# Output projection's steps spread around the last recurrent head, one memory key pair ahead of a norm, rotary work in pairs

## What is computed

```python
for i in range(2):                       # first block
    a = rms_norm(h, pre_mix_norm[i])
    m = hgrn2_mixer(a, ...) if i == 0 else mla_mixer(a, ...)
    h = h + rms_norm(m, post_mix_norm[i])
    f = squared_relu_mlp(rms_norm(h, pre_mlp_norm[i]), w_mlp_in[i], w_mlp_out[i])
    h = h + rms_norm(f, post_mlp_norm[i])
    e = p[i] @ w_ple_proj[i]             # the "embedding" of layer i
    h = h + rms_norm(sigmoid(h @ w_ple_gate[i]) * e, ple_norm[i])
# second block: hybrid mixer, cross attention to mem (256 rows), gated conv MLP
# hgrn2_mixer, per head of 8: q, two forget gates, v, output gate; a chunked scan both ways,
#   o = rms_norm(o_f + o_b) * silu(gate); then the heads together @ w_out
# mla_mixer: cq, ckv, k_rope = split(x @ w_in); cq, ckv normed
#   q = cq @ w_uq -> 16 heads of 128 + 64 rotary columns; k, v = ckv @ w_ukv
#   softmax(q_nope k_nope + q_rope k_rope) v, then the 16 heads @ w_o
```

## Time and profile before

| | |
|---|---|
| median of 3 runs (2368.69 to 2370.6) | 2370.27 us |
| the profiled execution's own time | 2372.49 us |
| its span | 2370.6 us |
| PE, share of the span busy | 97% |
| DVE, ACT, POOL | 54%, 27%, 66% |
| mean granted clock of PE | 0.989 |

### The profile page before, as it was taken

How to read it: one execution, slowest core, us unless ns; L and a number is a source line. 1 busy time by engine, 2 the same in 40 slices (tenths; PEclk the granted TensorE clock), 3 DMA queues, 4 the chain that set the end, 5 groups by cost and what they waited for, 6 DMA issues and landing times.

```text
span 2370.6 us, 27451 instructions
## 1 busy us (share of the span) xinstructions
PE 2291.2 (97%) x10372; PEld 1857.8 (78%) x10372; DVE 1271.2 (54%) x1820; ACT 648.5 (27%) x1190; POOL 1568.0 (66%) x1530
## 2 busy tenths in 40 slices
PE   7999989999999899999999999999999999999998
PEld 6888877888887677777778888878767787888886
DVE  6674727145245666256372454458875444626354
ACT  3343433101013345245231010132345232202112
POOL 7556556877776545544668777769425947878784
PEclk9999999999999899999999999999999999999999
DMA  5222222333332211211324333323212322333332
GB/s 162 76 71 80 72 79 73 112 97 97 98 98 76 59 35 36 71 42 32 97 73 128 98 99 111 98 76 116 71 37 80 111 67 89 96 97 97 98 96 73
DMA packets 110868, 200.13 MB, mean 84 GB/s; under 512 B 12305, under 2 KB 18705, under 8 KB 110737
## 3 DMA queue, kind: packets, MB, share of 16 engines
q1 hardware_dynamic: 107568, 194.72, 27.4%
q10 hardware_dynamic: 3168, 3.67, 0.5%
HBM read 196.24 MB, written 2.10 MB: 84 GB/s over the span
## 4 chain that ended last, share of the span: by engine, by line
PE 87%; DVE 6%; POOL 4%; ACT 2%; issue 1%; DMA 0%; SPq 0%; DVEq 0%; POOLq 0%
PE bank L469 26%; PE bank L471 25%; PE bank L470 25%; POOL wL L2612 2%; POOL wH L2610 1%; DVE bank L1834 1%; DVE h L1826 1%; PE bank L998 1%; PE bank L502 1%; PE bank L864 1%; DVE tmp L1826 1%; PE bank L869 1%; PE bank L870 1%; PE bank L865 1%; PE bank L866 1%
## 5 line engine op out<-in xcount | busy, mean ns | idle before, releaser
L2612 POOL TENSOR_TENSOR wL<-raw,wH 128x512 fp32r<-128x512 f32 (+2 forms) x731 | 1000.7, 1369 | 60.9
L2610 POOL TENSOR_SCALAR wH<-raw 128x512 fp32r<-128x512 f32 (+2 forms) x731 | 531.2, 727 | 616.4 <-PE bank L471 523.6
L469 PE MATMUL bank<-aH,wH 128*128 128x512 f32 x1376 | 547.0, 398 | 19.2 <-DVE aL L1834 9.6
L471 PE MATMUL bank<-aH,wL 128*128 128x512 f32 x1376 | 537.5, 391 | 0.0
L470 PE MATMUL bank<-aL,wH 128*128 128x512 f32 x1376 | 537.4, 391 | 0.0
L469 PE MATMUL bank<-uH,wH 128*128 128x512 f32 x960 | 375.7, 391 | 5.6 <-DVE uL L1826 5.6
L470 PE MATMUL bank<-uL,wH 128*128 128x512 f32 x960 | 374.5, 390 | 0.0
L471 PE MATMUL bank<-uH,wL 128*128 128x512 f32 x960 | 374.5, 390 | 0.0
L469 PEld LDWEIGHTS bank<-aH,wH 128*128 128x128 f32 x1376 | 258.9, 188 | 78.7 <-issue 13.1
L470 PEld LDWEIGHTS bank<-aL,wH 128*128 128x128 f32 x1376 | 259.0, 188 | 57.0 <-issue 4.1
L471 PEld LDWEIGHTS bank<-aH,wL 128*128 128x128 f32 x1376 | 258.9, 188 | 54.7
(11 more groups left out here) (315 smaller groups left out, 3202.3 us busy)
## 6 DMA issues: line engine op xcount, KB each, us to landing
raw<-in_ws SPq DMA_DIRECT2D x699, 256.0 KB, 2.6
raw<-in_ws SPq DMA_DIRECT2D x24, 192.0 KB, 2.3
h<-in_xT SPq DMA_DIRECT2D x4, 512.0 KB, 7.3
E<-in_memT ACTq DMA_DIRECT2D x16, 128.0 KB, 2.6
out<-c_F SPq DMA_DIRECT2D x8, 256.0 KB, 2.1
tmp<-in_pT ACTq DMA_DIRECT2D x4, 256.0 KB, 3.2
raw<-in_ws SPq DMA_DIRECT2D x8, 128.0 KB, 2.1
g_hc<-in_cst SPq DMA_DIRECT2D x1, 640.0 KB, 9.2
```

The costliest lines, as they stand in the source:

```text
L469: P.e.matmul(o, lH, rH, start=start, stop=False, skip_group_check=skip)
L471: return P.e.matmul(o, lL, rH, start=False, stop=stop, skip_group_check=skip)
L2610: G.e.tensor_scalar(H, x, 1.0, 0.0, MUL, ADD).then_inc(*G.did("wH", n))
L2612: G.e.tensor_tensor(L, x, H.bitcast(F32), SUB).then_inc(*G.did("w", n))
```

## The change

For head 7, one step of the output projection stands ahead of `recur(7)`, two ahead of `outputs(7)`, one behind it, and four behind the sum of squares; ACT loads the Exp table right after the last Sigmoid, ahead of its part of `recur(7)`. At the end of both embeddings tile 7 is squared by DVE; in layer 1 `memory_keys(0)` stands ahead of `stat_end` and `memory_keys(2)` behind it. In the attention's start, ACT squares the query latent into `m_P` and DVE adds the squares there, so the key latent's norm and the query latent's sum interleave; all `normed` run one tile ahead of their low halves; the rotary key comes last. `values_in(0)` stands ahead of the duplication; the query of head 0 ahead of its key; the rotary columns of heads 2 and 3 ahead of `scores(0)`, whose four banks are taken at once, all parts without rotary columns first. Rotary pairs come in odd iterations, one iteration earlier; `rotate` on DVE is cut in two, `rotate` and `rotated`, the latter in the next iteration, and `m_qr` is double buffered. Head 8's query, key and scores stand ahead of `mla_out(0)`, and the keys of heads 8 and 9 come as pieces of their own.

```diff
--- before.py
+++ after.py
     def keys(hd):
-        add("mla_w_ukv", 0, (0, 1), ((256 * hd, 128), (256 * hd + 256, 128)))
+        if hd in (8, 9):
+            add("mla_w_ukv", 0, (0, 1), cols((256 * hd, 128)))
+        elif hd % 2 == 0:
+            add("mla_w_ukv", 0, (0, 1), ((256 * hd, 128), (256 * hd + 256, 128)))
...
     values(0)
-    keys(0)
     rope(0)
     query(0)
+    keys(0)
+    rope(2)
     for hd in range(16):
...
-        if hd % 2 == 0 and hd < 14:
-            rope(hd + 2)
+        if hd % 2 and hd < 12:
+            rope(hd + 3)
         if hd % 8 == 7:
-            divided[len(out) + 1] = hd - 1
-            divided[len(out) + 5] = hd
-            mla_out(hd // 8)
+            divided[len(out) + (hd == 15)] = hd - 1
             if hd == 7:
                 head(8)
+            divided[len(out) + (5 if hd == 15 else 2)] = hd
+            mla_out(hd // 8)
...
                     lin = three_open([("hg_w_out", 0, 128 * o) for o in range(3)], ...
-                    for k in range(5):
-                        three_step(lin, k, uH, uL, y1_ready)
+                    out_steps(0)
                 recur(head)
                 if head < 7:
                     project(head + 1, 0)
                 else:
-                    three_step(lin, 5, uH, uL, y1_ready)
-                    three_step(lin, 6, uH, uL, y1_ready)
+                    out_steps(1, 2)
                 outputs(head)
                 if head < 7:
                     project(head + 1, 3)
+                else:
+                    out_steps(3)
                 stat_end("hs", head, tiles=1, tail=False, freed=(V, "on", head))
...
-            three_step(lin, 7, uH, uL, y1_ready)
+            out_steps(4, 5, 6, 7)
...
+                if i == 1:
+                    memory_keys(0)
                 stat_end("ple", i, adds=f"n{i}")
                 P.also("end ple", i)
                 if i == 1:
-                    for o in (0, 2):
-                        memory_keys(o)
+                    memory_keys(2)
...
+            values_in(0)
             b1, b2 = take("kr1"), take("kr2")
...
-            values_in(0)
-            key_in(0)
             rope_in(0)
             query_in(0)
             rotate(0)
+            key_in(0)
+            rope_in(2)
             scores(0)
             for hd in range(16):
-                ahead, turn = hd % 8 != 7, hd % 2 == 0 and hd < 14
+                ahead, turn = hd % 8 != 7, hd % 2 == 1 and hd < 12
                 if ahead:
                     heads_in(hd + 1)
                 if turn:
-                    rope_in(hd + 2)
+                    rope_in(hd + 3)
                 turned(hd)
                 if ahead:
                     scores(hd + 1)
+                elif hd == 7:
+                    heads_in(8)
                 if turn:
-                    rotate(hd + 2)
+                    rotate(hd + 3)
+                elif hd == 0:
+                    rotate(2)
                 values(hd)
                 if hd == 7:
+                    scores(8)
                     mla_out(0)
-                    heads_in(8)
-                    scores(8)
...
                 sigmoid_g(head)
                 if head < 7:
                     sigmoid_f(head + 1, 1)
+                else:
+                    exp_table()
                 recur(head)
...
-                    if o == 7:
-                        exp_table()
-                    A.wait_ge(V, "Fg", i, o)
-                    square(("ple", i), o, F[:, o, :])
+                    if o < 7:
+                        A.wait_ge(V, "Fg", i, o)
+                        square(("ple", i), o, F[:, o, :])
+                exp_table()
...
+                V.wait_ge(V, "Fg", i, 7)
+                V.wait_ge(V, "sum", ("ple", i), 6)
+                tt(sq[:, :], F[:, 7, :], F[:, 7, :], MUL).then_inc(*V.did("sq", ("ple", i), 7))
...
+            add_query_squares(1)
+            normed(3)
+            add_query_squares(2)
+            normed(4)
+            normed_low(3)
+            normed_low(4)
             V.wait_ge(P, "kr")
             tt(F[0:64, 5, :], bk("kr")[0:64, :], r[0:64, :], MUL).then_inc(*V.did("kr"))
-            for k in range(3):
-                normed(k, turned_key(k))
...
+            normed(0)
+            normed(1)
+            normed_low(0)
+            normed(2)
+            normed_low(1)
+            normed_low(2)
+            turned_key()
```

More of the change, by code:

```diff
@@ L366, in build @@
             m_qnH, m_qnL, m_knH, m_knL = (sb(n, [128, T], FR, st) for n in ("m_qnH", "m_qnL", "m_knH", "m_knL"))
-            m_qr = [sb(f"m_qr{i}", [128, T], FR, st) for i in range(2)]
+            m_qr = [[sb(f"m_qr{j}{i}", [128, T], FR, st) for i in range(2)] for j in range(2)]
             m_P = [sb(f"m_P{i}", [128, 4, T], F32, st) for i in range(2)]
@@ L815, in pe @@
             P.also("n0 used")
-            stat_end("cq", tiles=3, tail=False, freed=(V, "cn", 2))
+            b = take("stat", "cq")
+            P.wait_ge(V, "sum", ("cq",))
+            P.e.matmul(b.ap[:, :], ones, m_P[0][:, 0, :], start=True, stop=True).then_inc(*P.did("stat", "cq"))
+            give(b, V, "cn", 2)
             aVH, aVL, aPH, aPL = aH[:, 0:4, :], aL[:, 0:4, :], aH[:, 4:8, :], aL[:, 4:8, :]
@@ L1473, in act, with query_square @@
                 square(("ckv",), k, F[:, 3 + k, :])
-            rstd(256, "ckv")
+            def query_square(k):
+                A.wait_ge(V, "lat", k)
+                do(m_P[0][:, k, :], F[:, k, :], ACT.Square).then_inc(*A.did("sq", ("cq",), k))
             def latent(k):
@@ L1478, in latent @@
                 do(m_cH[:, k, :], tmp[k % 2][:, :], ACT.Copy).then_inc(*A.did("cH", k))
[L1480 to L1484 removed]
+            query_square(0)
+            query_square(1)
+            rstd(256, "ckv")
+            query_square(2)
+            latent(3)
+            latent(4)
             rstd(384, "cq")
@@ L1497, in values_in, with key_high @@
                     do(aVH[:, t, :], bk("mV", quad, t)[:, :], ACT.Copy).then_inc(*A.did("mVH", quad, t))
+            def key_high():
+                A.wait_ge(V, "kr3")
+                do(m_krH[:, :], F[:, 6, :], ACT.Copy).then_inc(*A.did("krH"))
             def rope_in(hd):
@@ L1549, in act @@
             values_in(0)
-            head_in(0, "kn", m_knH)
+            key_high()
             rope_in(0)
             head_in(0, "qn", m_qnH)
-            rotate(0)
-            A.also("rope done")
+            head_in(0, "kn", m_knH)
+            rotated(0)
             scores(0)
+            rope_in(2)
             for hd in range(16):
-                ahead, turn = hd % 8 != 7, hd % 2 == 0 and hd < 14
+                ahead, turn = hd % 8 != 7, hd % 2 == 1 and hd < 12
                 if ahead:
@@ L1564, in act @@
                     scores(hd + 1)
-                if turn:
-                    rotate(hd + 2)
+                elif hd == 7:
+                    heads_in(8)
+                if hd % 2 == 0 and 0 < hd < 14:
+                    rotated(hd + 2)
                 values(hd)
+                if hd == 0:
+                    rotated(2)
                 if hd == 7:
+                    scores(8)
                     A.wait_ge(V, "krL")
@@ L2271, in dve @@
             values_in(0)
-            head_in(0, "kn", m_knH, m_knL)
+            V.wait_ge(A, "krH")
+            low(m_krL[:, :], F[:, 6, :], m_krH[:, :]).then_inc(*V.did("krL"))
             head_in(0, "qn", m_qnH, m_qnL)
             rotate(0)
+            head_in(0, "kn", m_knH, m_knL)
+            rotated(0)
             scores(0)
             for hd in range(16):
-                ahead, turn = hd % 8 != 7, hd % 2 == 0 and hd < 14
+                ahead, turn = hd % 8 != 7, hd % 2 == 1 and hd < 12
                 if ahead:
@@ L2282, in dve @@
                     scores(hd + 1)
+                elif hd == 7:
+                    heads_in(8)
                 if turn:
-                    rotate(hd + 2)
+                    rotate(hd + 3)
+                elif hd == 0:
+                    rotate(2)
+                elif hd % 2 == 0 and hd < 14:
+                    rotated(hd + 2)
                 values(hd)
+                if hd == 0:
+                    rotated(2)
                 if hd == 7:
-                    heads_in(8)
                     scores(8)
```

117 lines of the change are left out of this document (62 added, 55 removed).

## The result

The changed kernel takes 2339.21 us (median of 4 runs, 2337.48 to 2340.41), the kernel before 2370.43 beside it (2368.69 to 2372.69): ratio 0.9867, 95% interval 0.985 to 0.9884, so 31 us less. The forecast was 2340.5. The profiled execution took 2338.12 (span 2336.3, mean granted clock 0.994) against 2372.49 before.

A forecast was written before the change was run, and what follows sets the result against it. PE bounds the kernel, busy 2291 of 2371 us, so only its waits and half-clock time can be won. Terms 3.4 - 0.3 + 14.0 + 6.3 + 5.9 + 0.5 = 29.8 us gave a 2340.5 us median; range 2332 to 2350.

The forecast's parts named there:

- Step 1: End of the recurrence: two PE waits and their half clock go, a new 4.1 us wait comes; net gain 3.4 us.
- Step 2: Square of the embeddings' last tile, on DVE in layer 0: 0.1 us gain to 0.7 loss, taken as 0.3 lost.
- Step 3: Attention's start: PE's waits and half clock, 14.8 us together, go against 0.8 us of new waits; net gain 14.0 us.
- Steps 4 and 5: Head loop: waits for `m_knL` in odd iterations shrink, gain 6.3 us; iteration 7's wait and half clock go, gain 5.9.
- step 5: Iteration 7: `values(7)`'s 4.3 us wait and 1.6 of clock loss go, by head 8's matmuls and no preceding `m_qr`; 5.9 us.
- Step 6: Second embedding: `memory_keys(0)` covers the square's wait, but POOL's splits set PE's restart; gain 0.5 us, bounds -1.5 and +1.
- B: Attention's start: DVE's chain is slower beside POOL's splits, `knL` 4 us later; 2347 us, chance 0.11.
- C: Attention's start: fp32 products, not waits, cause the low clock, so 5.0 us are not won; 2345.5 us, chance 0.11.
- D: POOL's divisions come later behind regrouped splits, delaying each `turned(hd)`; slower, 2379.5 us at 7 us each, chance 0.02.
- E: No change: head 7's new wait and the head loop's shifted ones return all but iteration 7; 2366 to 2370 us, chance 0.03.

The follow-up runs named there:

- square_alone: The changed kernel with one GpSimd weight piece in layer 0's embedding waiting for DVE's last-tile square; first embedding's stage 71.24 us against 72.97.
- table_later: The changed kernel with ACT's Exp table load behind its part of `recur(7)`; wait for `g_kT` 3.99 to 2.57 us, recurrence's stage 1.42 us shorter.
- steps_3_1_1_3: The changed kernel with the later Exp table load and output projection steps 3 | 1 | 1 | 3; recurrence's stage 76.3 us against 81.4.
- steps_alone: The changed kernel with output projection steps 3 | 1 | 1 | 3 and nothing else; recurrence's stage 76.52 us, 4.85 less.
- rec_only: The kernel before with only the change of the recurrence's end; 2368.13 us against 2371.69.
- values_behind: The changed kernel with PE's `values_in(0)` behind the two duplications of the rotary key; attention's stage 357.90 us, to the hundredth the changed kernel's.
- rotate_whole: The changed kernel with `rotated` right behind the rotation in odd iterations, not one iteration later; attention's stage 4.1 us longer.
- head8_late: The changed kernel with head 8's query, key and scores behind the first output projection again; attention's stage 1.97 us longer.
- keys_behind: The changed kernel with both `memory_keys` behind the second embedding's sum; second embedding's stage 175.49 us, ratio to the kernel before 0.9875.

## Why the prediction was right, step by step

The sum was 29.8 us, the medians moved by 31.2 and the profiled executions by 34.4, of which 1.9 lie ahead of any edit.

- **Step 1, 3.4, measured 4.0.** The wait is there as worked out (4.1, measured 3.99), for `g_kT`, with the table load ahead of the copy; the waits for the sum and for `uL` are gone. The clock cost 1.7 instead of 2.1 (the window of 0.57: low for 3.44 of 4 us). In three of the nine executions with this stage as in after it cost 1.1 to 1.3 more, so 2.7 to 4.0 is the part's worth, against the one R of before.
- **Step 2, -0.3, measured -1.5. This is the term that was mis-sized.** The square was placed right (763.03, behind the product) and its duration was within the bounds (1.64, upper bound 1.70), but of the two neighbouring rows the loss was taken near the middle. The rows part the 1.5: PE's wait for the square grew from 1.77 to 2.38 us, which is 0.6 and inside the forecast's bound of 0.7; and the clock fell ahead of two fp32 products, which took 2.02 us for 1.12, 0.9 more. The term had no clock in it at all. In `square_alone` both are gone; in `table_later`, `steps_3_1_1_3` and `steps_alone` the 0.6 stays and the 0.9 doesn't come, with the same square.
- **Step 3, 14.0, measured 15.2 or 14.4.** `turned(0)` starts at 853.05 before and 833.46 after, 19.6 less, of which 4.4 stand already at the landmark before it. Against `rec_only`, where the clock fell later, it is 14.4. Half clock and waits went as forecast, and of the 0.8 us of new waits only 0.2 came (`m_P`, at `turned(0)`), since DVE was ahead: `knL` ended at 825.06, when the first score was issued at 825.37. `values_behind` corrects the reason: the forecast credited `values_in(0)` with hiding the query latent's chain, and behind the duplications it hides as much.
- **Steps 4 and 5, 12.2, measured 14.0.** The places were right, all seven waits for `m_knL` and the one for `aL` are gone. The size was low because a wait costs more than its row: three waits of 3.4 us in `rotate_whole` cost A 4.1, one of 1.5 in `head8_late` cost 2.0. The products come every 0.23 us but their rows are 0.39 long, so the idle time in front of one begins 0.16 late, and the second product behind a wait comes 0.30 behind the first (865.73 and 866.03 in `rotate_whole`), 0.07 more. So 0.23 us for each wait: the three of `rotate_whole` cost 1.41, 1.30 and 1.44 for rows of 1.18, 1.04 and 1.18, and over eight waits it makes the 1.8. (Of head8_late's 0.5 it explains half.) In step 5 the credit was divided wrongly: the cover of head 8 had no part in the 4.3 us, and the `m_qr` halves did precede the low half, only earlier.
- **Step 6, 0.5, measured 0.35.** That GpSimd's splits set the restart was right. The size agrees, but K varied from 176.3 to 177.9 in kernels with the same code in it, so 0.35 us can't be given to the split of the keys, and `keys_behind` doesn't support it.
- **Rivals.** B: DVE's operations on two SBUF inputs were indeed slower at places (`m_cL`, two in 1.87 us at 806.17), but the chain had room. C: the clock was 1.00 from 812 to 824 with six fp32 products in it (814.81 to 816.7, and 821.02) and no wait ahead of them, so such products alone don't bring it down. D: no wait for `m_P` above 0.2. E: nothing was given back.

That the median came within 1.3 us of the forecast is in part luck: errors of -1.2 and +3.6 us met, and the stretches that nobody touched move a time by more than what was left; the single profiled execution was 4.6 below its own forecast of 2342.7.

## What to carry to other kernels

Count what stands ahead of the late operation on its own engine before looking for cover: the `m_qr` halves were fixed there, and the query squares too as far as the runs show, and PE's reordering beside them bought nothing (`values_in(0)`) or little (head 8, 2.0 us). Where PE's order is the remedy, size it by the late chain: two steps more ahead of `recur(7)`, 18 products of 0.225 us, covered 4.0 us of wait. Compare edits of a few microseconds by the lengths of the stages they touch, since untouched stages alone moved the total by up to 4.6 us. A stage's length repeats to 0.1 us where the clock falls at the same point (A 357.84 to 357.92 in nine executions), and differs by 0.9 to 3.3 us where it doesn't.

## What the runs showed of the hardware that was not expected

- The same wait, in the same place, is followed by half clock in some executions and not in others: 1.99 us for `uL` cost 0 in four profiled executions of fourteen, and 1.6 to 3.3 us in ten. The wait of 4.0 us for `g_kT` was followed by 1.2 GHz in all nine executions that have it, in three of them already from ahead of the restart, which costs 1.2 us more.
- Where the fall lands matters as much as that it comes: two fp32 products behind a wait of 2.3 to 2.4 us took 2.0 us in six executions and 1.12 in three, with the same code in the stage, and the stage went with it (E1 72.9 to 73.1 or 72.1).
- The same DVE product of two SBUF inputs took 0.69 us alone and 1.64 beside one GpSimd subtraction.
- A switch of ACT's table cost its load alone: the sigmoid ended at 297.44, the load took 1.28 us, the copy began at 298.75, so 1.3 us between them. The page "ScalarE: Activation LUTs" of the Trainium skill, section "What ACT_TABLE_LOAD costs", gives the load the same 1.28 us but a drain of 1.38 besides; by it PE's new wait would have been about 5.4 us, and the trace shows 3.99.
